# The second block's output projection as seven block products instead of thirty-two full-width matmuls

## The reference, cut to what matters

```python
def hybrid_layer(x, ...):                       # x: 256 x 1024
    h = rms_norm(x, norm_mix); proj = h @ w_in  # 256 x 2336
    oa = neighbourhood_attention(...)           # 6 heads: columns 0..383 of the mixer's output
    ob = latent attention (...)                 # 6 heads: 384 columns
    oc = gated short convolution (...)          # 256 columns
    o  = each of the three groups rms-normed by itself, times out_norm
    x  = x + o @ w_out                          # 256 x 1024 @ 1024 x 1024   <- the change
    h  = rms_norm(x, norm_ffn)
    # 16 experts, each takes the 32 tokens with the highest affinity softmax(h @ w_router + b_router)
    x  = x + sum of the experts' (silu(h @ w_gate) * (h @ w_up)) @ w_down, weighted
```

## Time and profile before

| | us |
|---|---|
| median of three runs | 1926.46 (1926.03 to 1927.03) |
| the profiled execution's own time | 1926.92 |
| its span | 1925.1 |
| PE busy | 1643.8 (85%) |
| DVE busy | 764.6 (40%) |
| ACT busy | 313.8 (16%) |
| GpSimd busy | 182.2 (9%) |

### The profile page before, as it was taken

How to read it: one execution, slowest core, us unless ns; L and a number is a source line. 1 busy time by engine, 2 the same in 40 slices (tenths; PEclk the granted TensorE clock), 3 DMA queues, 4 the chain that set the end, 5 groups by cost and what they waited for, 6 DMA issues and landing times.

```text
span 1925.1 us, 25329 instructions
## 1 busy us (share of the span) xinstructions
PE 1643.8 (85%) x10768; PEld 941.6 (49%) x10768; DVE 764.6 (40%) x1502; ACT 313.8 (16%) x823; POOL 182.2 (9%) x175
## 2 busy tenths in 40 slices
PE   8999999999999999999776766757999785756757
PEld 3455999444589964574332232322474432232322
DVE  1586788877738886663010100102573010010101
ACT  1243111021521101262000000001252000010000
POOL 0001034000215410310000000000210000000000
PEclk9999999999999999999897987879999897897978
DMA  9992998434454743546999999999746999999998
GB/s 356 330 355 91 330 334 279 153 131 175 135 189 169 263 153 125 184 181 274 415 432 428 427 434 423 434 428 402 243 175 255 403 428 432 425 434 425 432 429 351
DMA packets 165960, 599.81 MB, mean 312 GB/s; under 512 B 20976, under 2 KB 79856, under 8 KB 142064
## 3 DMA queue, kind: packets, MB, share of 16 engines
q1 hardware_dynamic: 165630, 598.04, 79.2%
q10 hardware_dynamic: 242, 0.53, 0.1%
HBM read 594.76 MB, written 3.80 MB: 311 GB/s over the span
## 4 chain that ended last, share of the span: by engine, by line
PE 55%; DMA 38%; DVE 4%; ACT 2%; issue 1%; POOL 0%; SPq 0%; DVEq 0%; ACTq 0%; POOLq 0%
DMA extra<-in_w_down 14%; DMA extra<-in_w_up 13%; DMA extra<-in_w_gate 11%; PE ps L1393 7%; PE ps L1420 7%; PE ps L1747 5%; PE ps L1347 5%; PE ps L1018 4%; PE ps L1187 4%; PE ps L1464 4%; PE ps L1629 3%; PE ps L1289 3%; PE ps L1495 2%; PE ps L1767 1%; DVE extra L2548 1%
## 5 line engine op out<-in xcount | busy, mean ns | idle before, releaser
L1747 PE MATMUL ps<-ring,wide 128*32 128x256 f32 x2912 | 226.2, 478 | 123.9 <-DMA ring<-in_w_up 79.4
L1747 PEld LDWEIGHTS ps<-ring,wide 128*32 128x32 f32 x2912 | 109.5, 136 | 233.9 <-DMA ring<-in_w_up 89.0
L3446 DVE TENSOR_TENSOR wide<-ps,wide 128x512 f32<-128x512 f32 x16 | 10.7, 670 | 506.1 <-PE ps L1747 506.1
L1767 PE MATMUL ps<-ring,wide 128*32 128x512 f32 x768 | 158.4, 641 | 47.7 <-DMA ring<-in_w_down 44.0
L1747 PE MATMUL ps<-extra,wide 128*32 128x256 f32 x1056 | 87.1, 499 | 55.9 <-DMA extra<-in_w_up 31.8
L1767 PEld LDWEIGHTS ps<-ring,wide 128*32 128x32 f32 x768 | 42.2, 117 | 159.8 <-issue 127.6
L1393 PE MATMUL ps<-hT,ring 128*128 128x128 f32 x960 | 114.7, 275 | 0.0
L1393 PEld LDWEIGHTS ps<-hT,ring 128*128 128x128 f32 x960 | 111.0, 192 | 1.0 <-issue 1.0
L1347 PE MATMUL ps<-hT,ring 128*128 128x128 f32 (+1 forms) x704 | 100.2, 304 | 0.0
L2315 ACT ACTIVATE wide<-ps 128x512 f32<-128x512 f32 x8 | 4.8, 597 | 566.5 <-PE ps L1767 425.3
L1347 PEld LDWEIGHTS ps<-hT,ring 128*128 128x128 f32 x704 | 94.0, 191 | 5.8 <-issue 1.0
(11 more groups left out here) (399 smaller groups left out, 2364.5 us busy)
## 6 DMA issues: line engine op xcount, KB each, us to landing
ring<-in_w_gate SPq DMA_DIRECT2D x24, 4096.0 KB, 31.3
ring<-in_w_down SPq DMA_DIRECT2D x24, 4096.0 KB, 33.2
ring<-in_w_up SPq DMA_DIRECT2D x20, 4096.0 KB, 32.7
ring<-in_w_mod SPq DMA_DIRECT2D x24, 2048.0 KB, 12.9
ring<-in_w_up SPq DMA_DIRECT2D x44, 1024.0 KB, 9.5
extra<-in_w_gate SPq DMA_DIRECT2D x8, 4096.0 KB, 35.1
extra<-in_w_up SPq DMA_DIRECT2D x8, 4096.0 KB, 33.0
ring<-in_w_in SPq DMA_DIRECT2D x13, 2048.0 KB, 9.8
```

The lines of the kernel that those rows point to most:

```text
L1747: last = mm(ps[2 * part + e // 2][j * CAP:(j + 1) * CAP, e % 2 * 2 * P:(e % 2 + 1) * 2 * P], xsT[:, k, e * CAP:(e + 1) * CAP], expert_row( ...
L1767: last = mm(ps[6 + n][e * CAP:(e + 1) * CAP, :], hidT[:, e, k, :], expert_row(n0, e, k)[:, n * N:(n + 1) * N], start=k == 0, stop=k == KD - 1)
```

## The change

The product of 256 x 1024 by 1024 x 1024 is split in 2 x 2 blocks: H[c][e] with token half c and half e of the contraction, W[e][n] with column half n. Four sums of rows and four sums of weights are made:

s3 = H00 - H10, s1 = H10 + H11, s2 = s1 - H00, s4 = H01 - s2; t3 = W11 - W01, t2 = t3 + W00, t4 = t2 - W10, t1 = W11 - t2.

Seven products of four matmuls each follow: M1 = H00 W00, M7 = s3 t3, M2 = H01 W10, M6 = s2 t2, M3 = s4 W11, M5 = s1 t1, M4 = H11 t4. The blocks of the result are M1 + M2 (0,0), M1 + M6 + M5 + M3 (0,1), M1 + M6 + M7 - M4 (1,0) and M1 + M6 + M7 + M5 (1,1). In the program h[c][e] and w[e][n] are overwritten by sums in place.

GpSimd makes t3 behind the taps; DVE makes the other sums and adds the products to x. The FAR group's root is now applied before the transposes (`far_scale`), on DVE. ACT copies M1 out of PSUM (out2_u), DVE adds M6 to that copy, and the sum goes into three blocks. The rows of w_out_2 are stored in another order, so that each half of the contraction is contiguous. The last product (M4) frees both weight slots. The router's matmul for c = 0, the transposes of the second column half of c = 1 and the logits of c = 0 now stand behind the last product.

```diff
+OUT2_STEPS = (1, 7, 2, 6, 3, 5, 4)
+OUT2_BANK = {1: 4, 7: 5, 2: 2, 6: 0, 3: 1, 5: 3, 4: 6}
+OUT2_SUMS = ("s3", "t2", "s1", "s2", "s4", "t4", "t1")
+OUT2_NEEDS = {1: (), 7: ("s3",), 2: (), 6: ("s2", "t2"), 3: ("s4",), 5: ("s1", "t1"), 4: ("t4",)}
...
+OUT2_ROWS = [k for _, k in sorted((at_, k) for k, at_, _ in NEAR + FAR)]
...
+        def out2_weights():
+            v = [slot2(B2_AT[("out", n)]).rearrange("p (e g m) -> p e g m", e=2, g=4) for n in range(2)]
+            return [[v[n][:, e, :, :] for n in range(2)] for e in range(2)]
+        def out2_rows():
+            v = hT[:, :].rearrange("p (e g c t) -> p e c g t", e=2, g=4, c=2)
+            return [[v[:, e, c, :, :] for e in range(2)] for c in range(2)]
+        out2_s3 = spare[:, 2048:2560].rearrange("p (g t) -> p g t", g=4)
+        out2_u = sm[:, 2, :]
+        def out2_done(s, L, m):
+            if m == 4:
+                return tile_done, b2_used(L, B2_AT[("out", 1)])
+            return s.at("block_product_done", len(IN2_STEPS) + OUT2_STEPS.index(m))
...
-                def out2(bank, parts, c, n, some=slice(None)):
-                    wt = slot2(B2_AT[("out", n)]).rearrange("p (k n) -> p k n", k=KD)
-                    for k, at_, _ in parts[some]:
-                        last = mm(ps[bank][:, :], h8[:, at_, c * P:(c + 1) * P], wt[:, k, :],
-                                  start=k == parts[0][0], stop=k == parts[-1][0])
-                    return last
+                def block_out(m, some=range(4)):
+                    if some[0] == 0:
+                        if m == 7:
+                            pe.wait_ge(*s.at("b2_taps_ready", 2))
+                        for name in OUT2_NEEDS[m]:
+                            pe.wait_ge(*out2_sum(s, name))
+                    w, h = out2_weights(), out2_rows()
+                    lhs, rhs = {1: (h[0][0], w[0][0]), 2: (h[0][1], w[1][0]), 3: (h[0][1], w[1][1]), 4: (h[1][1], w[1][0]),
+                                5: (h[1][0], w[0][0]), 6: (h[0][0], w[0][0]), 7: (out2_s3, w[0][1])}[m]
+                    for g in some:
+                        last = mm(ps[OUT2_BANK[m]][:, :], lhs[:, g, :], rhs[:, g, :], start=g == 0, stop=g == 3)
+                    if some[-1] == 3:
+                        if m == 4:
+                            last.then_inc(tile_done, 2)
+                        else:
+                            last.then_inc(s.up("block_product_done"), 1)
                 for n in range(2):
                     pe.wait_ge(*b2_loaded(L, B2_AT[("out", n)]))
                 pe.wait_ge(*s.at("b2_out_by_act", 2))
                 pe.wait_ge(*s.at("b2_out_by_dve", 1))
-                out2(4, NEAR, 0, 0).then_inc(s.up("b2_out_done"), 1)
-                pe.wait_ge(*s.at("att_out_read", MAPS2))
+                block_out(1)
+                block_out(7, range(0, 2))
+                pe.wait_ge(*s.at("b2_mixed_ready", 2))
                 for i, (_, _, col) in enumerate(FAR):
                     for c in range(2):
                         o = ((i + 1) % 2) * T + c * P
                         last = nc.tensor.transpose(ps[6 + (i + 1) // 2][:, o:o + P], proj2[:, c, col:col + P], ident)
                     if i in (0, 2):
                         last.then_inc(s.up("b2_out_flipped"), 1)
-                out2(5, NEAR, 0, 1).then_inc(s.up("b2_out_done"), 1)
-                out2(0, NEAR, 1, 0).then_inc(s.up("b2_out_done"), 1)
-                out2(1, NEAR, 1, 1).then_inc(s.up("b2_out_done"), 1)
+                block_out(7, range(2, 4))
+                pe.wait_ge(*s.at("b2_proj_by_act", 7))
                 pe.wait_ge(*s.at("b2_out_by_act", 3))
                 pe.wait_ge(*s.at("b2_out_by_dve", 2))
-                out2(2, FAR, 0, 0).then_inc(s.up("b2_out_done"), 1)
-                out2(3, FAR, 0, 1).then_inc(s.up("b2_out_done"), 1)
+                block_out(2)
+                block_out(6)
+                block_out(3)
...
-                        pe.wait_ge(*s.at("b2_mixer_added", 2 * c + hf + 1))
+                        pe.wait_ge(*s.at("b2_mixer_added", (1, 2, 4, 3)[2 * c + hf]))
...
-                out2(6, FAR, 1, 0, slice(0, 2))
-                flip_rows(0)
-                out2(6, FAR, 1, 0, slice(2, 3)).then_inc(tile_done, 1)
-                out2(7, FAR, 1, 1, slice(0, 2))
+                flip_rows(0, (0,))
+                block_out(5)
+                block_out(4, range(0, 2))
+                flip_rows(0, (1,))
+                block_out(4, range(2, 4))
                 pe.wait_ge(sems["router_loaded"], 16 + DEPTH)
                 pe.wait_ge(sems["pads_cleared"], 4)
                 pe.wait_ge(*s.at("b2_x_by_act", 3))
                 pe.wait_ge(*s.at("b2_x_by_dve", 3))
                 route(0).then_inc(s.up("b2_router_done"), 1)
-                out2(7, FAR, 1, 1, slice(2, 3)).then_inc(tile_done, 1)
+                flip_rows(1, (1,))
+                logits(0)
                 flip_rows(1, (0,))
-                logits(0)
-                flip_rows(1, (1,))
+                pe.wait_ge(*s.at("b2_x_by_act", 4))
+                route(1, range(4, KD), 1)
                 pe.wait_ge(*s.at("b2_x_by_dve", 4))
-                route(1, range(0, 4))
-                pe.wait_ge(*s.at("b2_x_by_act", 4))
-                route(1, range(4, KD)).then_inc(s.up("b2_router_done"), 1)
+                route(1, range(0, 4), 1).then_inc(s.up("b2_router_done"), 1)
...
+                act.wait_ge(*out2_done(s, L, 1))
+                av(out2_u, ps[OUT2_BANK[1]][:, :], ACT.Copy).then_inc(s.up("b2_proj_by_act"), 1)
...
+                ffn_squares(1, 1)
+                router_copy(0)
                 ffn_squares(1, 0)
-                router_copy(0)
-                ffn_squares(1, 1)
...
+                for n in range(2):
+                    pool.wait_ge(*b2_loaded(L, B2_AT[("out", n)]))
+                w = out2_weights()
+                gp.tensor_tensor(w[0][1], w[1][1], w[0][1], ALU.subtract).then_inc(s.up("b2_taps_ready"), 1)
...
-                def near_add(c, n):
-                    dve.wait_ge(*s.at("b2_out_done", 2 * c + n + 1))
-                    xv = x[:, c, n * N:(n + 1) * N]
-                    tt(xv, ps[4 - 4 * c + n][:, :], xv, ALU.add).then_inc(s.up(), 1)
-                def far_add(c, n):
-                    if c == 0:
-                        dve.wait_ge(*s.at("b2_out_done", n + 5))
+                xh = [[x[:, c, n * N:(n + 1) * N] for n in range(2)] for c in range(2)]
+                w, h = out2_weights(), out2_rows()
+                def far_scale():
+                    dve.wait_ge(*s.at("b2_mixed_rstd", 2))
+                    for c in range(2):
+                        v = proj2[:, c, CQ2:CQ2 + 384]
+                        ts(v, v, rsm[1][:, 3 * c + 2:3 * c + 3], None, ALU.mult)\
+                            .then_inc(s.up("b2_mixed_ready" if c else None), 1)
+                def rows3(name):
+                    if name == "s3":
+                        dve.wait_ge(*s.at("b2_out_by_act", 2))
+                    elif name == "s1":
+                        dve.wait_ge(*s.at("b2_out_by_act", 3))
                     else:
-                        dve.wait_ge(tile_done, b2_used(L, B2_AT[("out", n)]))
-                    xv = x[:, c, n * N:(n + 1) * N]
-                    stt(xv, ps[2 + 4 * c + n][:, :], rsm[1][:, 3 * c + 2:3 * c + 3], xv, ALU.mult, ALU.add)\
-                        .then_inc(s.up("b2_mixer_added"), 1)
+                        dve.wait_ge(*out2_done(s, L, {"s2": 1, "s4": 2}[name]))
+                    dve.wait_ge(*s.own())
+                    out_, p, q, op = {"s3": (out2_s3, h[0][0], h[1][0], ALU.subtract), "s1": (h[1][0], h[1][0], h[1][1], ALU.add),
+                                      "s2": (h[0][0], h[1][0], h[0][0], ALU.subtract),
+                                      "s4": (h[0][1], h[0][1], h[0][0], ALU.subtract)}[name]
+                    tt(out_, p, q, op).then_inc(s.up("block_sum_ready"), 1)
+                def weights3(name):
+                    dve.wait_ge(*out2_done(s, L, {"t2": 1, "t4": 2, "t1": 6}[name]))
+                    if name == "t2":
+                        dve.wait_ge(*s.at("b2_taps_ready", 2))
+                    else:
+                        dve.wait_ge(*out2_sum(s, {"t4": "t2", "t1": "t4"}[name]))
+                    out_, p, q, op = {"t2": (w[0][0], w[0][1], w[0][0], ALU.add),
+                                      "t4": (w[1][0], w[0][0], w[1][0], ALU.subtract),
+                                      "t1": (w[0][0], w[1][1], w[0][0], ALU.subtract)}[name]
+                    tt(out_, p, q, op).then_inc(s.up("block_sum_ready"), 1)
+                def product_add(m, c, n, name=None, op=ALU.add):
+                    dve.wait_ge(*out2_done(s, L, m))
+                    dve.wait_ge(*s.own())
+                    tt(xh[c][n], xh[c][n], ps[OUT2_BANK[m]][:, :], op).then_inc(s.up(name), 1)
+                def shared_add():
+                    dve.wait_ge(*out2_done(s, L, 6))
```

(51 more changed lines are left out.)

10 lines of the change are left out of this document (5 added, 5 removed).

## The result

The changed kernel takes 1914.9 us (median of 4 runs, 1914.39 to 1916.08) against 1926.31 for the kernel before (1926.03 to 1927.03): ratio 0.9941 [0.9926, 0.9956], 11.4 us faster. Two later comparisons of the same two kernels gave gains of 9.1 (0.9952 [0.9939, 0.9966]) and 10.1 us (0.9942 [0.9928, 0.9956]), so about 10 us is the size to explain, and the forecast's sum was 6.8.

The account below looks back on a forecast made before the run. It took PE to bound the output projection and the weight stream to bound the expert stages. The routing chain's 3.4 us in each of two layers made 6.8 us, forecast 1919.6 us, range 1917.8 to 1922.2.

Parts of the forecast that it names:

- the forecast's sum: Whole kernel: two layers, each gaining the routing chain's 3.4 us, give 6.8 us.
- What PE does: Output projection: four matmuls less (3.43 us) and the router's eight moved (0.57) bring the last product's end 4.0 us earlier.
- DVE beside PE: Output projection: all 13 us of new DVE work lies beside PE, which never waits; narrowest slack 0.3 us.
- rival B: Output projection: DVE takes PE's place at narrow points, PE waits 2.0 us, a layer gains 1.4: 1923.7 us; chance 0.10.
- C: Weight stream: transfers hide the gain, through SP's queue or a start fixed by bytes; no change, 1926.5 us; chance 0.04.
- t3 on GpSimd: Attention, before the projection: the sum takes 5.1 us (bounds 3.7 to 7.3), hidden in GpSimd's idle time, cost nothing.
- Rival D: Attention: t3 on GpSimd stops DVE's masks for its whole length; 4.8 us slower, 1931.3 us; chance 0.04.
- The row parts: Transfers issued behind the experts' first matmuls, at 908.01 in the first layer: to come 3.4 us earlier a layer.
- The layout: Projection's end and routing: small mean, exponential and ACT's router copy placed 3.4 us earlier, within 3.1 to 4.0.
- The stream: Experts' weights: queue already dry at 908, so the later release (3.4 us) counts and the gap grows by 0.6.
- the first shift: Weights for slots 0 and 1, issued when the output projection has read those slots: 4.0 us earlier a layer.
- The forecast's list of what would prove it wrong: Signs: PE idle ahead of M2 or M5, masks over 0.7 us, a later first matmul, or DMA share 1.0 before the row parts.

Follow-up runs that it names:

- t3_dve: Changed kernel with t3 made by DVE behind s3 instead of by GpSimd in the attention: 1917.86 us, 0.9959 of the kernel before.
- before_again: The kernel before, no edit, profiled a second time: 1925.38 us, ratio 0.9997.
- less4: The kernel before with one of five chunks left out of the NEAR sums, four projection matmuls less a layer: 1918.74 us, ratio 0.9964.
- after_hold: Changed kernel with the weights for slots 0 and 1 held until the router's matmul of token half 0: 1918.7 us, 0.9962 of the kernel before.
- after_split: Changed kernel with slot 1's half of the weights for slots 0 and 1 issued early, behind M3 and t1: 1913.99 us, 0.9943 of the kernel before.
- after_best: Changed kernel with slot 1's weights issued early and token half 0's logits behind the last transposes: 1915.0 us, 0.9939 of the kernel before.
- before_split: The kernel before with slot 0's half of the weights for slots 0 and 1 issued early: 1922.5 us, ratio 0.9982.

## Why the prediction was wrong

Point by point:

- What PE does. Four matmuls and the router's eight out of the way of the last product: 4.0 forecast, 4.20 measured. Four matmuls at the stretch's mean, (30.04 - 0.66 - 0.87 - 0.57) / 32 = 0.873, are 3.49 and not 3.43; the other 0.14 I did not trace.
- DVE beside PE. Right: no wait of PE on DVE, rival B did not come. Nor did C: the stream did follow what moved.
- t3 on GpSimd. Right: 4.53 us, hidden; on DVE the same sum costs 1.6 us (t3_dve). Rival D did not come: the mask beside t3 took 0.69 us, as the earlier trace rows has it without.
- The row parts. 3.4 forecast, 3.55 measured. The layout followed the small mean and the exponential, and they come 3.28 and 3.31 us earlier (890.04 and 890.57 now); ACT's copy of the router's sums, which was to follow with the same shift, comes 3.54 earlier (890.88), and the row parts 3.55.
- The stream. This is the step that failed: "As the queue runs dry at 908 already, the later one counts, and the gap grows by 0.6." It had not run dry. The window 908 to 911 gave a share of 0.84, and I read the missing 0.16 of 3 us as a gap ahead of the row parts. Cut finer, the same stretch of the kernel before reads:

```profile
907.01:908.01 1.00, 1.00 (x21) 0.42 (x14) 0.00 (x0) 0.00 (x0) 0.00 (x0) 1.00 0.95 377
...
908.01:909.01 1.00, 1.00 (x12) 0.88 (x14) 0.00 (x0) 0.00 (x0) 0.00 (x0) 1.00 0.95 393
909.00:910.00 1.00, 1.00 (x21) 0.65 (x24) 0.61 (x2) 0.00 (x0) 0.00 (x0) 1.00 0.75 209
```

On both sides of the issue at 908.01 the share is 0.95: the older transfers were still on their way, 0.5 MB of them, and the dip comes a microsecond later, with the row parts already issued. So the first shift, which the sum left out, had a price of its own: it brought the queue from 0.5 MB left to 0.2. That was worth about 1.7 us a layer beside the row parts' 3.55, as the stages show:

The stages of all thirteen profiles, two each, fall in two groups by what is left of the 6.3 MB when the row parts are issued (from windows as above; the distance is from the last issue into slots 0 and 1, and the piece is the stream's second-to-last):

| kernels | us between the issues | MB left | MB moved up to 15 us behind the issue | piece behind the issue, us |
|---|---|---|---|---|
| before, before_again, less4, after_hold (8 stages) | 14.97 to 14.99 | 0.48 to 0.58 | 10.76 to 11.34, mean 11.07 | 420.1 to 422.7, mean 421.3 |
| all others (18 stages) | 15.61 and more; with one half early 15.61 (after_split), 15.37 (after_best), 14.97 (before_split) | 0 to 0.35 | 11.43 to 11.60, mean 11.54 | 419.4 to 420.6, mean 419.6 |

The groups differ by 1.7 us a layer; single stages overlap (420.1 and 420.5 in the first, 420.6 in the second). before_split keeps the distance of the first group and empties the queue, and its stages lie with the second. 2 x (3.55 + 1.7) = 10.5 us, where 11.4, 9.1 and 10.1 were measured. The 1.7 is a difference found behind the result and not worked out from a mechanism. What the first comparison has above 10.5 lies within the size of the scatter of the program's start and of single late pieces. The forecast's list of what would prove it wrong named a DMA share of 1.0 ahead of the row parts, by which the gain would be the first shift's. The share was there (0.95); the gain is neither shift's, but the later one's and 1.7 us.

The range was too narrow for this reason alone: it took the end of the stream as a fixed distance behind one issue, and left no room for what the queue does in between.

## What to carry to other kernels

Whether a queue is dry is read at the very moment of the next issue, in windows of 1 us or by adding up the bytes moved against the bytes issued, never from a mean over several. Where two releases of one stream move by different amounts, price the change of their distance as well as the later one. Between DVE and GpSimd, ask of a large sum in SBUF what small operation of the other engine it would hold up, not only whether its own engine is idle.
